# An mLSTM whose value tiles carry a column of ones and whose row of maxima comes back from memory, with a new order in the mixer's first slabs

## The reference

```python
logw = b[..., :, None] - b[..., None, :] + it[..., None, :]   # causal, else -1e30
m_t = jnp.maximum(b + m[..., None], jnp.max(logw, axis=-1))
scores = jnp.einsum('bhtd,bhsd->bhts', qt, kt) * jnp.exp(logw - m_t[..., None])
num = w_inter[..., None] * jnp.einsum('bhtk,bhvk->bhtv', qt, C) + jnp.einsum('bhts,bhsv->bhtv', scores, vt)
den = w_inter * jnp.einsum('bhtk,bhk->bht', qt, n) + jnp.sum(scores, axis=-1)
h = num / jnp.maximum(jnp.abs(den), jnp.exp(-m_t))[..., None]
C_new = decay[..., None, None] * C + jnp.einsum('bhs,bhsv,bhsk->bhvk', ws, vt, kt)
n_new = decay[..., None] * n + jnp.einsum('bhs,bhsk->bhk', ws, kt)
```

## Time and profile before

| what | value |
|---|---|
| median of three executions | 2470.65 us |
| profiled execution, its span | 2470.8 us, 2469.0 us |
| TensorE matmuls busy | 2444.2 us, 99% |
| VectorE, ScalarE busy | 1068.7 us (43%), 766.8 us (31%) |
| mean granted TensorE clock | 0.997 of full |
| DMA, mean share of 16 engines | 0.30 |

### The profile page before, as it was taken

How to read it: one execution, slowest core, us unless ns; L and a number is a source line. 1 busy time by engine, 2 the same in 40 slices (tenths; PEclk the granted TensorE clock), 3 DMA queues, 4 the chain that set the end, 5 groups by cost and what they waited for, 6 DMA issues and landing times.

```text
span 2469.0 us, 27519 instructions
## 1 busy us (share of the span) xinstructions
PE 2444.2 (99%) x11756; PEld 2037.1 (83%) x11756; DVE 1068.7 (43%) x1566; ACT 766.8 (31%) x1128; POOL 17.1 (1%) x16
## 2 busy tenths in 40 slices
PE   8999999999999999999999999999999999999998
PEld 7888888778888888888888888887788888888887
DVE  3333246455555553332443332554555556433324
ACT  3222123344343232221232221233444332322211
POOL 0000200000000000000000000000000000000000
PEclk9999999999999999999999999999999999999999
DMA  5332234222223323332233232342232223332232
GB/s 179 103 103 89 104 100 128 77 78 85 86 69 103 137 88 100 102 100 91 100 103 103 86 102 103 99 129 69 69 100 72 85 103 119 103 103 89 100 108 81
DMA packets 204970, 243.40 MB, mean 99 GB/s; under 512 B 10288, under 2 KB 166960, under 8 KB 204848
## 3 DMA queue, kind: packets, MB, share of 16 engines
q1 hardware_dynamic: 204848, 241.63, 29.7%
HBM read 235.31 MB, written 6.29 MB: 98 GB/s over the span
## 4 chain that ended last, share of the span: by engine, by line
PE 99%; DVE 1%; DMA 0%; ACT 0%; issue 0%; SPq 0%; DVEq 0%
PE main L1247 22%; PE main L1249 21%; PE main L1248 21%; PE main L1345 5%; PE main L1347 4%; PE main L1346 4%; PE side L1346 4%; PE side L1345 4%; PE side L1347 4%; PE main L1328 1%; PE main L1329 1%; PE main L1330 1%; PE side L1270 1%; PE side L1500 1%; PE side L1462 1%; PE side L1486 0%
## 5 line engine op out<-in xcount | busy, mean ns | idle before, releaser
L1247 PE MATMUL main<-xh,wh 128*128 128x512 f32 x2128 | 839.1, 394 | 5.8 <-DVE mvt L942 5.8
L1248 PE MATMUL main<-xh,wl 128*128 128x512 f32 x2128 | 831.0, 391 | 0.0
L1249 PE MATMUL main<-xl,wh 128*128 128x512 f32 x2128 | 830.7, 390 | 0.0
L793 DVE TENSOR_TENSOR wl<-raw,wh 128x1024 fp32r<-128x1024 f32 (+2 forms) x440 | 498.6, 1175 | 722.1 <-ACT wh L526 721.7
L526 ACT ACTIVATE wh<-raw 128x1024 fp32r<-128x1024 f32 (+2 forms) x440 | 423.7, 1012 | 703.4 <-PE main L1249 305.5
L1247 PEld LDWEIGHTS main<-xh,wh 128*128 128x128 f32 x2128 | 400.7, 188 | 96.4 <-DVE mvt L942 7.5
L1249 PEld LDWEIGHTS main<-xl,wh 128*128 128x128 f32 x2128 | 400.7, 188 | 84.8
L1248 PEld LDWEIGHTS main<-xh,wl 128*128 128x128 f32 x2128 | 401.0, 188 | 81.4 <-issue 0.5
L896 DVE SCALAR_TENSOR_TENSOR hp<-main,sil 128x512 f32<-128x512 f32 x88 | 56.7, 686 | 306.3 <-PE main L1249 297.1
L587 ACT ACTIVATE hh<-hp 128x512 fp32r<-128x512 f32 x88 | 54.1, 632 | 353.3 <-DVE hp L896 353.3
L1345 PE MATMUL main<-wh,hh 128*128 128x512 f32 x352 | 137.7, 391 | 0.0
(11 more groups left out here) (232 smaller groups left out, 2280.0 us busy)
## 6 DMA issues: line engine op xcount, KB each, us to landing
raw<-gu SPq DMA_DIRECT2D x176, 512.0 KB, 4.5
raw<-w_in SPq DMA_DIRECT2D x100, 512.0 KB, 4.6
raw<-down SPq DMA_DIRECT2D x80, 512.0 KB, 4.2
raw<-w_branch SPq DMA_DIRECT2D x24, 512.0 KB, 4.1
raw<-w_out SPq DMA_DIRECT2D x16, 512.0 KB, 4.1
raw<-w_in SPq DMA_DIRECT2D x28, 256.0 KB, 3.4
raw<-down SPq DMA_DIRECT2D x16, 256.0 KB, 2.8
spill<-xt SPq DMA_DIRECT2D x8, 512.0 KB, 6.2
```

The source lines that it names most:

```text
L793: ins = V.tensor_tensor(put(wl[slot]), get(raw[slot]), f32(put(wh[slot])), ALU.subtract)
L1247: T.matmul(out, hi, rh(k), start=k == 0, stop=False)
L1248: T.matmul(out, lo, rh(k), start=False, stop=False)
L1249: ins = T.matmul(out, hi, rl(k), start=False, stop=k == kk - 1)
```

## The change

Values and states get a 129th column. `mvt` becomes [128, 4 chunks, 4 heads, 129] with ones in the last column (a memset in each layer), `CS` becomes three states of 129 columns, and `NS` is gone. Each pair of a 128-column and a one-column matmul becomes one matmul of 129 columns; results lie 129 apart in the banks, the fourth numerator in bank 3. VectorE and ScalarE read them there: `mem2` loses its three operations on `NS`, `mem3` has three small copies in place of two, ScalarE's copy of the numerators becomes two (384 and 128 columns).

The rows of maxima no longer go through `row_of` (VectorE, 16x512) and the matmul with ones. SyncE stores `rg` to memory after slab 9's load and loads one head's four rows, 2 KB, into all 128 partitions (`gb`, 256 KB written): head 0's after slab 12's load, the others' after the load of slabs 21, 24 and 27, once `Dm` of the head before is made. `mem1` makes `Dm` from `gb` before it waits for TensorE.

In the first slabs tile 1 of slab 0 comes before tile 0 of slab 1; in ScalarE's `norm_tail`, `root` of tile 3 comes before `high` of tile 2; the rotary matmul of the keys moves from the end of slab 5 to its middle; VectorE empties the first bank of slab 5 before `rope` of the keys, not after.

The buffers above `mvt` move by a quarter of a kilobyte a partition, and `mtmp` to another place. The core of the diff:

```diff
-        mvt = big("mvt", 28, [P, NB, WB])
+        mvt = big("mvt", 28, [P, NB, MH, P + 1])
-        CS = big("CS", 8, [P, 3, P])
+        CS = big("CS", 8, [P, 3, P + 1])
-        rowx = tmp("rowx", 4, [16, NB, P])
+        gb = tmp("gb", 4, [P, NB, P])
...
+                    if s == 9:
+                        sp.wait_ge(g_rows.sem, g_rows.val(layer, 1))
+                        sp.dma_start(grows[layer], rg[:, :]).then_inc(grows_out.sem, 16)
+                    if s in (12, 21, 24, 27):
+                        h = max(0, (s - 18) // 3)
+                        if h:
+                            sp.wait_ge(dm_ready.sem, dm_ready.val(layer, h))
+                        else:
+                            sp.wait_ge(grows_out.sem, 16 * (layer + 1))
+                        sp.dma_start(gb[:, :, :], grows[layer].rearrange("(n h) t -> h n t", h=MH)[h].partition_broadcast(P)).then_inc(
+                            gb_in.sem, 16)
...
                     split(g + 2)
-                    high(L + 1, 2)
                 root(L, 3)
                 if L < NORMS - 1:
+                    high(L + 1, 2)
                     high(L + 1, 3)
...
             def mem1(layer, h):
-                dve.wait_ge(m1_ps.sem, m1_ps.val(layer, h + 1))
+                dve.wait_ge(gb_in.sem, gb_in.val(layer, 16 * h + 16))
                 mt = const[:, K_MT:K_MT + P].unsqueeze(1).broadcast_to([P, NB, P])
-                V.scalar_tensor_tensor(out=Dm[:, :, :], in0=n4(sd[:, 1, :]), scalar=-1.0, in1=mt,
+                V.scalar_tensor_tensor(out=Dm[:, :, :], in0=gb[:, :, :], scalar=-1.0, in1=mt,
                                        op0=ALU.mult, op1=ALU.add).then_inc(*o.up(dm_ready))
+                dve.wait_ge(m1_ps.sem, m1_ps.val(layer, h + 1))
...
                     if s == 5:
+                        rows_out(layer, NB)
                         rope(layer, 4, kT[:, :], 0)
-                        for i in range(NB, 2 * NB):
+                        for i in range(NB + 1, 2 * NB):
                             rows_out(layer, i)
...
                 tile_of(0, 0)
+                tile_of(1, 0)
+                turn_tile(v, 2)
                 tile_of(0, 1)
-                turn_tile(v, 2)
-                tile_of(1, 0)
                 tile_of(1, 1)
...
                 if s == 5:
+                    rotate(layer, 4, kT[:, :], 0, 4)
                     pe.wait_ge(carry.sem, carry.val(layer, 1))
...
-                        pe.wait_ge(rowx_ready.sem, rowx_ready.val(layer, h + 1))
-                        T.matmul(sd[:, 1, :], ones[0:16, :], rowx[:, :, :].rearrange("p n t -> p (n t)"), start=True, stop=True)
...
-                            T.matmul(sd[:, 0, c], mq[:, h, c], CS[:, n - 1, :], start=True, stop=True)
-                            ins = T.matmul(sd[:, 3, 4 + n:5 + n], mq[:, h, c], NS[:, n - 1:n], start=True, stop=True)
+                            ins = T.matmul(sd[:, 0, (P + 1) * (n - 1):(P + 1) * n], mq[:, h, c], CS[:, n - 1, :], start=True, stop=True)
...
-                        T.matmul(sd[:, 1, P * n:P * n + P], Dm[:, n, :], mvt[:, n, P * h:P * h + P], start=True, stop=True)
-                        T.matmul(sd[:, 3, n:n + 1], Dm[:, n, :], ones[:, 0:1], start=True, stop=True)
+                        out_ = sd[:, 1, (P + 1) * n:(P + 1) * n + P + 1] if n < 3 else sd[:, 3, 0:P + 1]
+                        T.matmul(out_, Dm[:, n, :], mvt[:, n, h, :], start=True, stop=True)
                     for n in range(NB - 1):
-                        T.matmul(sd[:, 2, P * n:P * n + P], kw[:, n, :], mvt[:, n, P * h:P * h + P], start=True, stop=True)
-                        ins = T.matmul(sd[:, 3, 8 + n:9 + n], kw[:, n, :], ones[:, 0:1], start=True, stop=True)
+                        ins = T.matmul(sd[:, 2, (P + 1) * n:(P + 1) * n + P + 1], kw[:, n, :], mvt[:, n, h, :], start=True, stop=True)
```

More of the change, by code:

```diff
@@ L55 @@
 K_ID, K_ONE, K_ROT, K_MASK, K_MT, K_FREQ = 0, 128, 256, 384, 640, 768
-K_HM = 769
-K_HALF_PI = K_HM + 16
+K_HALF_PI = 769
 K_EPS = K_HALF_PI + 1
@@ L112, in build @@
         mk = big("mk", 20, [P, MH, SEQ])
-        mvt = big("mvt", 28, [P, NB, WB])
[L114 to L120, removed]
+        mvt = big("mvt", 28, [P, NB, MH, P + 1])
+        cx = big("cx", 36.25, [P, 4, SEQ])
+        cc = big("cc", 44.25, [P, 4, SEQ])
+        cb = big("cb", 52.25, [P, 4, SEQ])
+        gt = big("gt", 68.25, [P, 4, SEQ])
+        yA = big("yA", 76.25, [P, 4, SEQ])
+        brow = big("brow", 68.25, [P, N_ROWS])
         ropetmp = big("ropetmp", 86, [P, SEQ])
         convtmp = big("convtmp", 86, [P, SEQ])
-        og = big("og", 44, [P, 4, SEQ])
+        og = big("og", 44.25, [P, 4, SEQ])
         yCl = big("yCl", 0, [P, 4, SEQ], F32R)
-        yCh = big("yCh", 60, [P, 4, SEQ], F32R)
+        yCh = big("yCh", 60.25, [P, 4, SEQ], F32R)
         yAl = big("yAl", 0, [P, 4, SEQ], F32R)
-        yAh = big("yAh", 60, [P, 4, SEQ], F32R)
-        yMh = big("yMh", 36, [P, 4, SEQ], F32R)
-        yMl = big("yMl", 52, [P, 4, SEQ], F32R)
+        yAh = big("yAh", 60.25, [P, 4, SEQ], F32R)
+        yMh = big("yMh", 36.25, [P, 4, SEQ], F32R)
+        yMl = big("yMl", 52.25, [P, 4, SEQ], F32R)
         mh = [big(f"mh{i}", (12, 20)[i], [P, 4, SEQ], F32R) for i in range(2)]
-        ml = [big(f"ml{i}", (28, 60)[i], [P, 4, SEQ], F32R) for i in range(2)]
-        CS = big("CS", 8, [P, 3, P])
+        ml = [big(f"ml{i}", (28, 60.25)[i], [P, 4, SEQ], F32R) for i in range(2)]
+        CS = big("CS", 8, [P, 3, P + 1])
         ytmp = big("ytmp", 10, [P, SEQ])
@@ L145, in build @@
         kbias = place("kbias", [P, MH])
-        NS = place("NS", [P, 3])
         cols = place("cols", [P, 5, 16])
@@ L182, in build @@
         rf, ri, rb, ra, rloc, rg, rm, rz = (tmp(f"row{i}", 0.5 * i, [16, P]) for i in range(8))
[L184 removed]
+        gb = tmp("gb", 4, [P, NB, P])
         Dm = tmp("Dm", 6, [P, NB, P])
         kw = tmp("kw", 8, [P, NB, P])
+        mtmp = tmp("mtmp", 10, [P, SEQ])
         numh = big("numh", 86, [P, NB, P])
@@ L192, in build @@
         sd = ctx.enter_context(nc.psum_tensor("side", [P, 4, SEQ], F32))
+        grows = nc.dram_tensor("grows", (DEPTH, 16, P), F32, kind="Internal").ap()
         spill = nc.dram_tensor("spill", (SEQ, D), F32, kind="Internal").ap()
@@ L292, in build @@
         o_used = Signal("o_used", 8)
-        rowx_ready = Signal("rowx_ready", MH)
+        grows_out = Signal("grows_out")
+        gb_in = Signal("gb_in", 16 * MH)
         m1_ps = Signal("m1_ps", MH)
@@ L921, in rope, with heads @@
                 o.settle()
+            def heads(a):
+                return a.rearrange("p (h c) -> p h c", h=2)
             def rows_out(layer, i):
@@ L934, in rows_out @@
                 ps = pm[t if first else (1, 0, 2, 3)[t]]
+                if i == 0:
+                    V.memset(mvt[:, :, :, P:P + 1], 1.0)
                 if first:
@@ L939, in rows_out @@
                     V.tensor_tensor(vtok[:, t, :], ps[:, 0:P], brow[:, 0:P], ALU.add)
-                    V.tensor_tensor(mvt[:, t, 0:256], ps[:, P + 8:N_VG], brow[:, P + 8:N_VG], ALU.add).then_inc(*o.up(rows_used))
+                    V.tensor_tensor(mvt[:, t, 0:2, 0:P], heads(ps[:, P + 8:N_VG]), heads(brow[:, P + 8:N_VG]), ALU.add).then_inc(*o.up(rows_used))
                 else:
-                    V.tensor_tensor(mvt[:, t, 256:512], ps[:, 0:256], brow[:, N_VG:N_ROWS], ALU.add).then_inc(*o.up(rows_used))
+                    V.tensor_tensor(mvt[:, t, 2:4, 0:P], heads(ps[:, 0:256]), heads(brow[:, N_VG:N_ROWS]), ALU.add).then_inc(*o.up(rows_used))
             def memory_gates(layer, s):
@@ L1022, in attn_pT @@
                 V.tensor_copy(pT[:, 1, :], sd[:, 3, :]).then_inc(*o.up(pT_dve))
[L1024 to L1028, removed]
             def of_head(kind, h):
@@ L1048, in mem2 @@
                 dve.wait_ge(m2_ps.sem, m2_ps.val(layer, h + 1))
-                V.tensor_copy(CS[:, 0, :], sd[:, 2, 0:P])
-                V.tensor_copy(NS[:, 0:1], sd[:, 3, 8:9]).then_inc(*o.up())
+                V.tensor_copy(CS[:, 0, :], sd[:, 2, 0:P + 1]).then_inc(*o.up())
                 for n in (1, 2):
                     o.settle()
[L1053 to L1057, removed]
+                    V.scalar_tensor_tensor(out=CS[:, n, :], in0=CS[:, n - 1, :], scalar=cols[:, 4, 4 * n + h:4 * n + h + 1],
+                                           in1=sd[:, 2, (P + 1) * n:(P + 1) * n + P + 1], op0=ALU.mult,
                                            op1=ALU.add).then_inc(*o.up(st_ready if n == 2 else None))
@@ L1063, in mem3 @@
                 dve.wait_ge(numl_ready.sem, numl_ready.val(layer, h + 1))
-                V.tensor_copy(dn[:, 0:4], sd[:, 3, 0:4])
-                V.tensor_copy(dn[:, 5:8], sd[:, 3, 5:8]).then_inc(*o.up())
+                V.tensor_copy(dn[:, 0:3], n3(sd[:, 1, :])[:, :, P])
+                V.tensor_copy(dn[:, 3:4], sd[:, 3, P:P + 1])
+                V.tensor_copy(dn[:, 5:8], n3(sd[:, 0, :])[:, :, P]).then_inc(*o.up())
                 for n in (1, 2, 3):
```

(10 more changed lines are left out.)

9 lines of the change are left out of this document (6 added, 3 removed).

## The result

The changed kernel takes 2427.8 us (2427.62 to 2427.87, four runs) against 2471.1 us (2470.32 to 2473.23, four runs): ratio 0.9823, interval 0.9806 to 0.9840. It is 43 us faster.

A forecast was written before the change was run, and what follows sets the result against it. TensorE was taken as the bound, its own work or waiting being the kernel's time. Savings of 10.5 + 3.8 + 22.0 = 36.3 us from the profiled 2470.8 us gave 2434.5 us, range 2430 to 2445.

The forecast's parts named there:

- The bound: Whole kernel: TensorE's matmuls busy 2444.2 of 2469.0 us; other engines cost only where TensorE waits for them.
- the pace: Main matmuls in slab 6 at full clock: 0.228 us each from start to start.
- part 1: Slab 6, both layers: wait for VectorE and half clock behind it go, 10.5 us saved.
- part 4: Work added on SyncE, VectorE and ScalarE, including the gb loads: cost to TensorE 0.
- Part 2: First slabs, both layers: the two waits of 1.91 us for wl go, 3.8 us saved.
- this second move: ScalarE's root of tile 3 ahead of high of tile 2: tile ready near 381.5 instead of 383.6.
- Part 3: TensorE in the mLSTM's eight heads: matmul of ones and ten one-column matmuls go, 2.75 us a head, 22.0 in all.
- I take 1.05, as that is its own place: Price of the removed 512-column matmul of ones in each head: 1.05 us, with 0.88 as lower bound.
- Rivals 1: Slab 6: rope and gate rows come too late on VectorE, wait and half clock stay; 2445 us, chance 0.06.
- 2: Heads: one-column matmuls ran in time that stays, their 13.6 us are not saved; 2448 us, chance 0.06.
- rival 3: Heads: rows of 129 elements stream slowly, each of 80 matmuls taking twice 0.25; 2454.5 us, chance 0.04.
- 5: Whole kernel: no difference, gains and new waits cancel; chance 0.02.

The follow-up runs named there:

- these two edits: Kernel before with only the keys' rotary matmul moved to the middle of slab 5 and its first bank emptied before rope: 2461.5 us against 2470.0, ratio 0.9962.

## Why the prediction was wrong, by its steps

**The bound, the pace, parts 1 and 4: right.** The clock went with the wait, no new wait came in the mixers, nothing added was on the path; the one new line of waits, 0.2 us, is at the kernel's start. Part 1 was 10.5 against 10.7. That is luck in part: the forecast and the 10.7 come from the same profile, with one of the two longest half clocks seen at slab 6. At full clock the stretch takes 29.26 us with the wait and 26.08 without, so 6.4 us of the 10.7 are the wait and 4.4 the clock (5.8 and 4.7 in the prediction), and by medians these two edits gave 8.4.

**Part 2: the size right, one reason wrong.** 3.8 against 4.3: the idle time was read from the row's bracket, where from start to start it is 2.1 to 2.2. "Without this second move 383.6 would be a new wait of 0.4 us" fell: `high`, and `root` behind it, wait for a transpose that the new order itself brings forward. In part 1 the order on VectorE was likewise not needed.

**Part 3: the step that failed.** It is "four matmuls of 128 columns without such a partner lie between 606.49 and 607.49: 0.25 each". That row was chosen as the clean price of a matmul alone, but it stands right behind the 16-row matmul, which slows it; without that it takes 0.89, 0.22 each. Both bounds of the term, 0.25 and 0.27, came from that one row, and so were no bounds. A partner's price is about half of the pair's 0.434: measured, ten of them save 2.28 us a head and not 1.7, 4.6 us of the 6.7 missing. The second failure is "I take 1.05, as that is its own place": the change from 128 rows to 16 and back also cost the neighbours 0.20, which is 1.6 us in all. The rest is part 2's 0.5.

**The rivals.** Rivals 1, 2, 3 and 5 did not come. Against rival 3, 129 columns with odd starts stream as 128 do (0.89 us from start to start for eight instructions with either, 598.48 to 599.37 and 605.30 to 606.19 above). The chance of 0.96 for faster was in the right place; the range was too narrow on the side of the gain.

## What to carry to other kernels

Where TensorE is the bound, count its instructions with a weight load of their own: here any float32 one behind 128 columns of weights costs 0.11 us up to 129 columns, so a one-column matmul is as dear as a full one, and a column of ones in the operand that streams gives row sums for no time that shows. Take the price of an instruction from two places, and never only from behind an instruction of another shape. Look at what a matmul does to the next one before its own length is called its cost, above all where the two use different numbers of rows, and count that loss once for a group of such matmuls.

## What the runs showed of the hardware

- A float32 matmul of 16 rows and 512 columns took 1.05 us, the same over 128 rows 0.86; four of 128 columns lost the same 0.19. What follows lost another 0.20 behind the 16-row ones, split matmuls and float32 ones alike. Ahead of weights of 16 or of 64 rows, behind those of 128, 0.35 us pass without a load.
- The clock after the same 2.90 us wait differed between executions and between layers, from no fall to over 6 us at 1.2 GHz. It also fell behind some of the 1.91 us waits in the first slabs and not behind others. The kernel before scatters by 4 us (2469.0 to 2473.2), the kernel after by 0.3 (2427.6 to 2427.9). That the clock behind the waits is the whole of this scatter is not shown: without the wait at slab 6 but with that in the first slabs, one run of four was 2.3 us below the others. The profiled one of those others lost 1.5 us to half clock behind the first slabs' wait; the low one was not profiled.
